# State passes of two mixers with their products grouped by rows, and a new order of steps for the second block

## What is computed

```python
def hgrn2_chunked(q, log_f, v):
    def step(state, inp):
        ...
        o = attn @ vt + jnp.einsum('bhtd,bhde->bhte', qt * jnp.exp(cum), state)
        ...
        state = jnp.exp(last[:, :, 0, :, None]) * state + jnp.einsum('bhsd,bhse->bhde', kt * jnp.exp(last - cum), vt)
        return state, o

def gated_delta_chunked(q, k, v, beta, g):
    def step(state, inp):
        u, w, qd, kd, qkc, gl = inp
        v_new = u - w @ state
        o = qd @ state + qkc @ v_new
        state = gl[..., None, None] * state + jnp.swapaxes(kd, -1, -2) @ v_new
        return state, o
```

## Time and profile before

| | |
|---|---|
| time, median of 3 runs | 4048.95 us (4043.9 to 4053.02) |
| the profiled execution | 4049.31 us, span of its instructions 4047.5 us |
| busy in that execution | PE 3833.2 us (95%), DVE 2624.0 (65%), ACT 1559.1 (39%), POOL 181.7 (4%) |
| mean granted PE clock | 0.968 of full speed |
| chain that ended last | PE 81%, DVE 11%, ACT 3%, DMA 2% |

### The profile page before, as it was taken

One profiled execution on the slowest core, in us unless ns is written; L12 is line 12 of the kernel. 1 busy time (PEld: TensorE's weight loads), 2 busy tenths in 40 slices (PEclk: granted clock), 3 DMA queues, 4 the chain that ended last, 5 costly groups with the idle time before them and its releaser, 6 DMA issues.

```text
span 4047.5 us, 49585 instructions
## 1 busy us (share of the span) xinstructions
PE 3833.2 (95%) x19548; PEld 3145.3 (78%) x19548; DVE 2624.0 (65%) x4164; ACT 1559.1 (39%) x2627; POOL 181.7 (4%) x335
## 2 busy tenths in 40 slices
PE   6889999998999999999989999999999989999998
PEld 5769878877788788887876788778888766887776
DVE  6887465655785522447778753776568788447865
ACT  3453232244532422334433343554334433335542
POOL 0000000000000000000111000000001110000010
PEclk9999899999998999999999999999899999999999
DMA  7502255532211332334444222134244442331233
GB/s 242 165 22 84 73 178 197 193 116 72 63 48 58 112 94 84 108 109 126 145 150 150 75 85 88 66 112 138 88 135 136 148 151 86 94 94 47 84 132 113
DMA packets 227128, 451.60 MB, mean 112 GB/s; under 512 B 18560, under 2 KB 63648, under 8 KB 225104
## 3 DMA queue, kind: packets, MB, share of 16 engines
q1 hardware_dynamic: 197584, 335.12, 25.6%
q0 software_dynamic: 29312, 113.32, 8.8%
HBM read 412.45 MB, written 35.93 MB: 111 GB/s over the span
## 4 chain that ended last, share of the span: by engine, by line
PE 81%; DVE 11%; ACT 3%; DMA 2%; issue 2%; SPq 0%; POOL 0%; DVEq 0%; ACTq 0%; POOLq 0%
PE ps L608 62%; PE ps L151 13%; PE ps L162 4%; DVE arena L173 3%; DVE arena L188 2%; ACT arena L247 2%; DVE spl L173 2%; DMA arena<-cumd 1%; DVE X L173 1%; DMA arena<-kvd 1%; PE ps L859 1%; DVE sm L194 1%; DVE arena L224 1%; PE ps L157 1%; ACT sph L247 0%
## 5 line engine op out<-in xcount | busy, mean ns | idle before, releaser
L173 DVE TENSOR_TENSOR spl<-ring,sph 128x1024 fp32r<-128x1024 f32 (+2 forms) x556 | 650.6, 1178 | 695.8 <-ACT sph L247 695.2
L247 ACT ACTIVATE sph<-ring 128x1024 fp32r<-128x1024 f32 (+2 forms) x556 | 558.5, 1018 | 692.4 <-PE ps L608 661.1
L608 PE MATMUL ps<-sph,HTh 128*128 128x512 f32 (+3 forms) x1680 | 666.0, 396 | 11.6 <-DVE HTl L173 5.0
L608 PE MATMUL ps<-spl,HTh 128*128 128x512 f32 (+3 forms) x1680 | 623.6, 371 | 0.0
L608 PE MATMUL ps<-sph,HTl 128*128 128x512 f32 (+3 forms) x1680 | 623.5, 371 | 0.0
L247 ACT ACTIVATE arena<-ps 128x512 f32<-128x512 f32 (+2 forms) x570 | 314.1, 564 | 763.4 <-PE ps L608 411.3
L608 PE MATMUL ps<-HTh,sph 128*128 128x512 f32 x1360 | 540.5, 397 | 11.3 <-ACT X L247 10.5
L608 PE MATMUL ps<-HTl,sph 128*128 128x512 f32 x1360 | 532.3, 391 | 0.0
L608 PE MATMUL ps<-HTh,spl 128*128 128x512 f32 x1360 | 532.3, 391 | 0.0
L151 PE MATMUL ps<-arena 128*128 128x128 f32 (+6 forms) x2264 | 369.6, 344 | 56.4 <-DVE arena L173 30.5
L608 PE MATMUL ps<-sph 128*128 128x512 f32 x992 | 400.5, 404 | 4.8 <-DVE spl L173 4.8
(11 more groups left out here) (218 smaller groups left out, 4898.8 us busy)
## 6 DMA issues: line engine op xcount, KB each, us to landing
ring<-in_w_in SPq DMA_DIRECT2D x264, 512.0 KB, 3.7
arena<-in_ada_w SPq DMA_DIRECT2D x88, 512.0 KB, 5.0
arena<-cumd POOLq DMA_DIRECT2D x128, 256.0 KB, 3.9
ring<-in_w_down SPq DMA_DIRECT2D x44, 512.0 KB, 3.7
ring<-in_w_gate SPq DMA_DIRECT2D x40, 512.0 KB, 3.7
ring<-in_w_up SPq DMA_DIRECT2D x40, 512.0 KB, 4.3
ring<-in_w_mem SPq DMA_DIRECT2D x32, 512.0 KB, 3.4
ring<-in_w_out SPq DMA_DIRECT2D x32, 512.0 KB, 3.6
```

The lines of the kernel that those rows point to most:

```text
L173: self.e.tensor_tensor(o, a, b, op).then_inc(*self.done.up())
L247: self.e.activation(o, a, f, **kw).then_inc(*self.done.up())
L608: ins = pe.e.matmul(o, l, r, start=k0 == 0 and i == 0 and not b.pairs, stop=k0 + b.ks == b.kt and i == 3 * b.ks - 1 and (c0 > 0 or not b.p ...
```

## The change

The functions `hgrn_pe` and `inv_pe` are changed, and the two strings of the second block. In both functions the products over 64 rows are taken together: the bank of the outputs is cleared by the product with one row of zeros, then come the two state products of the rows 0 to 63, then the four products over 128 rows, then the two of the rows 64 to 127, with a wait on the first two in place of `pe.own()`. In `inv_pe` the state part of the outputs moves ahead of the step of the weave, around `values_pe`, so that the bank og is taken earlier; after the step only the four state products and the four of G5 with VN are left. All sums have the same terms. The scores of "mix" stay as they are. The two strings of the second block have the same number of every letter but in another order.

```diff
     ("proj", 0):
-        "35McMdMd3Md8Md3M2d2Md2Mc4McMdc2Mcdc7M5c2M2dMcMsMcd2Mc5MscMdM2dMcdMdMc3Md6M2cMsdc2MdsMc4Mc2dcd2Mc2M2c"
...
+        "22Ms8Msd4M2d2McMcMcMd2Mc2Md5M2c5Md3Mc2dc3Md5Mc2dMc2dM2dcMc2Mcd2Mc3Md14M2c3Mc2McMdcMdsMdsd3c2MdMcdM2s"
...
     ("proj", 1):
-        "17Ms3MrMr2M2r7Msd6Md7MdMc6Mc3MdcMcMc2McMdcd2McMd5Md2MdM2cd3M2cd6Md3MdMcd2M2dcMcdMd2c5Md2McMc3Mc2d2sM"
...
+        "5M2r12Mr3Ms6Mr5Md4Mc7Mc3Mdc6MdMc2MdMcM2c2MdMc2Mc3Md3MdMd2Mdc2Md2c2M2dMd3Mc3M2c5Md3M2d2csc2MdMc3Mc3Md"
...
@@ hgrn_pe
+                    pe.e.matmul(b[:, 0:256], NFr[0][0:1, :], zero.to_broadcast([1, 256]), start=True, stop=False)
                     pe.wait_ge(at["st", l, c], at["lev_acc", l])
-                    for h in HO:
-                        pr, ti = (h % 2) * 64, h // 2
-                        hs = slice(64 * h, 64 * h + 64)
-                        if h == 1:
-                            pe.own()
-                        at["ob", l, c] = pe.mm(b[:, hs], [
-                            (ACC[:, c, h * 128:(h + 1) * 128], BV3[:, c, hs]),
-                            (BQ3[pr:pr + 64, ti, c * 128:(c + 1) * 128], STs[c % 2][pr:pr + 64, ti, :])])
+                    for half in range(2):
+                        if half:
+                            for h in range(4):
+                                hs = slice(64 * h, 64 * h + 64)
+                                pe.add(b[:, hs], ACC[:, c, h * 128:(h + 1) * 128], BV3[:, c, hs])
+                            pe.wait_ge(at["ob", l, c])
+                        for ti in range(2):
+                            pr, hs = 64 * half, slice(64 * (2 * ti + half), 64 * (2 * ti + half) + 64)
+                            at["ob", l, c] = pe.add(b[:, hs], BQ3[pr:pr + 64, ti, c * 128:(c + 1) * 128], STs[c % 2][pr:pr + 64, ti, :],
+                                                    stop=half + ti == 2)
@@ inv_pe
-                    if m < 3:
-                        values_pe(pe, l, m + 1)
+                    b2 = take(pe, ("og", l, m), pool("og"))
+                    pe.e.matmul(b2[:, 0:256], NFr[0][0:1, :], zero.to_broadcast([1, 256]), start=True, stop=False)
+                    for half in range(2):
+                        if half and m < 3:
+                            values_pe(pe, l, m + 1)
+                        pe.wait_ge(at["og", l, m] if half else None)
+                        for ti in range(2):
+                            pr, hs = 64 * half, slice(64 * (2 * ti + half), 64 * (2 * ti + half) + 64)
+                            at["og", l, m] = pe.add(b2[:, hs], QT_[pr:pr + 64, m, ti, :], SG[pr:pr + 64, ti, :])
                 yield (0.5, 0)
                 if m < 4:
-                    b2, b3 = [take(pe, (n, l, m), pool(n)) for n in ("og", "sg")]
+                    b3 = take(pe, ("sg", l, m), pool("sg"))
                     pe.wait_ge(at["vn", l, m])
...
-                    for h in HO:
-                        pr, ti = (h % 2) * 64, h // 2
+                    for h in range(4):
                         hs = slice(64 * h, 64 * h + 64)
-                        if h == 1:
-                            pe.own()
-                        at["og", l, m] = pe.mm(b2[:, hs], [
-                            (G5[:, m, h * 128:h * 128 + 128], VN[:, hs]),
-                            (QT_[pr:pr + 64, m, ti, :], SG[pr:pr + 64, ti, :])])
+                        at["og", l, m] = pe.add(b2[:, hs], G5[:, m, h * 128:h * 128 + 128], VN[:, hs], stop=h == 3)
```

More of the change, by code:

```diff
@@ new lines @@
+        "5Md5McsMdc2Md6McdcMd4Mc2MdMc2dMc2Md2Mcs2MsdMscdsMdMd4Ms2McMdMdMs3MdMc2McMd2s2Mc3McdMs2Md6Mcs3McMcdsc"
+        "dc2ds3Mc2Md3McMsdsc2Mc3Mdc4Ms4cMdMcMcscdMd2Md3M3dsMsdcMc2MsdM2c2Mc2Mc2dMdcs2M2sMsMs3MsMs4M2s2M2s3MsM"
+        "sMp3MsM2pMsM2psp3Ms3Mp2spsMp4Mps2MpMpM3ps2p2M2spMpMspMsMspMs2Ms2Mp2Mp2Msp2Mpsp2s5M3p2sMp3Mp2sMpMspMp"
+        "M2s2p2MsMspMpMsM2p2s2pMpM2p5Mpg3p2M4pM2p2MpMpM2pMpMpM2p2M3p2MgMpgM3p2MpM2p3MpM4pM3p4Mg19Mg4Mg4MgMg5M"
+        "g4MtMt2MtMt4Mg2MtM3tMt2Mt2M2t3Mt2Mt2M2t3Mt5Mt5MtMt2Mt2Mt2Mt3MtMt5Mt4Mt2Mt3Mt30M3t6Mt7Mf2M2f2MfMf5MfM"
@@ new lines @@
+        "2f2MfMf3Mf2Mf2MfMf3MfMfMfMfMf5MfMfMnfMf2M2f5Mn2Mf4MfMf3MnMf4Mf4MnMn2f2Mf2M2fM3fnxMnxyxMxyMxn2yxny2n"
+        "7M2yx4M2z2Mz2Mz4Mz29Mm12Mm2Mmsm3Mm28M",
+    ("proj", 1):
+        "5M2r12Mr3Ms6Mr5Md4Mc7Mc3Mdc6MdMc2MdMcM2c2MdMc2Mc3Md3MdMd2Mdc2Md2c2M2dMd3Mc3M2c5Md3M2d2csc2MdMc3Mc3Md"
+        "MdsMcMcdMdMsc3Ms3McdMd4MdMsd3MdMd2c3Mc2Mc3McdMcsd2cds2dcs5MdscMc3McsMcMd3Mscs6MdMs5Ms3d3Ms2d3Msd2sdc"
+        "McdMc4Msd3McMdMsd8MdMcMscMcMcMc2Mds3McMcMc2dcdMcMdMdsMc2dMdcMcd2MsdMcMsMcMdM3csMc2dsMs2M2s8MsMsMsMs"
+        "3M2s5M2s2p3MspMpsMpM2psMpMs2p2M2sMp2M2s2p6Msps2MpMpspMs2MpMsMpMrp3Mps2M2p2M2sp2MpMspMsM2p2Mp2s2M2p4M"
+        "sps3MpM2s2pMp2MpspsMpMs2ps8M4s2p2M2pM5pg3p2Mp3M2pg2pMpM3p5M2pMpM2pgpM3p2M2pgM5p2M3p14Mg7Mg5Mg9MgMt3M"
+        "t2MtMt4Mt2M3t4Mt4MtMt7M3tMtMt9Mgt3MtMt3M3t2Mt11MtMt2MtMt7MsM3t7Mt8Mg2Mt11Mt7M3f3Mf4Mf2MfMf2MfMfMf2Mf"
+        "MfMf2MfMfMf2MfMf2Mf2MfMf3Mnf4Mf5Mn2Mf4Mf3Mn2Mf3Mf2MfMf2MfMfn3MfnM2f3Mf3M3f2nx2MyMxnyx2ynx2n4Myx2My"
+        "10MxMyMx2M3zM2z26M2m17M2m4Mm25M",
```

10 lines of the change are left out of this document (removed).

## The result

| | before | after |
|---|---|---|
| time, median | 4047.99 us (4 runs) | 3999.15 us (3988.8 to 3999.68, 4 runs) |
| ratio | | 0.9873, 95% interval 0.9853 to 0.9892 |
| span of the profiled execution | 4047.5 us | 3997.2 us |
| mean granted clock in it | 0.968 | 0.974 |

What follows compares the result with a forecast made beforehand. PE was taken to bound the kernel, busy 95% of the span. Grouped products -8.5, scan order -12.9 and crowded pass steps +6.8 sum to -14.6 us: from 4049.3 to 4034.7, said as 4035 us, likely 4024 to 4045.

Steps and rivals of the forecast that it cites:

- (a): State passes: bank og is taken earlier, needing ACT's copy of the chunk before; 0.9 us to spare, costed at nothing.
- (b): State passes: PE needs DVE's next state; covered by 0.2 us only where no projection lies between; costed at nothing.
- (c): Grouped products: the wait on the first two is met, since five other products lie between (1.21 or 0.91 us).
- Part 1: Grouped products in hgrn and delta rule: about 0.5 us less in each of 16 chunks, -8.5 us with clock.
- the count: Second block's scan: 5.4 us row period minus PE's work, summed over short units from 8 on; 28.9 before, 16.0 after.
- Time saved on the other engines is worth nothing by itself: Whole kernel: an edit is worth only what it takes from PE's own stream or PE's waits.
- the relief of the scan: Second block's scan: the new orders cut the summed shortage from 28.9 to 16.0 us, worth -12.9 us.
- 28.9 against 43.5: Second block's scan: shortage counted before the change against PE time measured as empty in two windows, in us.
- the crowding: Second block's pass: steps beyond the second at a position go from 16 to 31, 0.45 us each, +6.8 us.
- part 1's tenth: Grouped products: a tenth added to 8.0 us because some chunks run at half clock, giving -8.5 us.
- Rival (A): Scan relieved in full: 19.4 us of waits, 6.5 of clock, 8.5 from grouped products; 4015 us, chance 0.2.
- the part on waits: Passage on waits that the grouped products add or move: three listed, costed at nothing, up to 3.6 us without cover.

## Why the prediction was wrong, point by point

**Right.** PE bounds the kernel, hgrn's chunk takes 2.89 us, the last block of the delta rule 1.3, and there are 16 instructions more. Layer 1 is the one that gained. The waits (a), (b) and (c) appear nowhere. The Trainium skill's rule (TensorEngine Tiling (Array Packing), Key Properties) that a change of the tiling mode drains the engine fits the chunk: 0.53 us less with four changes fewer.

**Right by luck.** Part 1: -8.5 were forecast, and -6.5 ± 2.4 measured at equal clock. But its halves, priced at some 4 us each, are not alike: hgrn's gives -7.7 ± 2.4, the delta rule's 1.2 ± 3.2 the wrong way. Layer 0: the count said -1.0, measured are 1.1 ± 3.3 for its string. Place by place it was otherwise, by the profiles of layer 1's string alone and of both strings, which differ in layer 0's string only: from position 100 to 285 the new one takes 11.6 us less, from 285 to 330 3.5 more, and from 453 on 9.1 more. So the stretch with the scan gained over ten times what was counted, and the tail, which the prediction had cost at nothing, lost most of it. (A slip without weight: the steps r move by up to 16 positions, not 15.)

**Wrong, other engines.** "Time saved on the other engines is worth nothing by itself" doesn't hold in the scan: 22 us less of work on DVE gave 11.2. PE's waits there are waits for DVE, and a shorter queue on DVE shortens them though none of them names the operation that went.

**Wrong, the relief of the scan.** The step "28.9 against 43.5 ... it catches the place, if not all of it" is where it failed. I left the 12.9 us as counted. In layer 1, 27.5 us were empty between 180 and 285 and 17.6 were counted, and the new order took 23.8 of the 27.5 away. 5.4 of them went in the window 180 to 214, mostly the convolution's end, where the count had no shortage at all; what else it missed lies in the scan, where the run with less work on DVE points to DVE's own queue. -29.7 at equal clock stand against -11.9 counted for that layer.

**Wrong, the crowding.** +6.8 us was charged and next to nothing of it came: the window with eight steps at one place has 0.1 us empty in layer 1, the one of layer 0 0.9. With 33 more steps beyond the second the price came out as 0.34 each (0.45 charged), so the term was of the right kind, but it doesn't start with the first step.

**Left out, the clock.** The forecast held no term for it outside of part 1's tenth. After runs at 0.9745 for 0.9690, 15 us, of which some 5 can be chance. One piece can be told: in layer 1's windows 13.6 us at 1.2 GHz are gone. A second is likely, in the first block: up to the first product of the second block the profiles hold 147 us at 1.2 GHz on average with the old functions (126 to 164, 11 profiles) and 132 with hgrn grouped (120 to 143, 7 profiles). The ranges overlap, so it rests on means, and the clock of whole executions doesn't settle it: beside the executions of before that belong to them, both mixers grouped lie 0.0039 higher and hgrn alone 0.0014. Rival (A) had a term for the clock, at 6.5 us for the scan, and full relief; it was the nearest with 4015 us, and it too was short, as it had neither the head of layer 1 nor a change of the clock in the first block.

**The new wait** of the transposes, 3.2 us, was missed in the part on waits: I had listed who needs the results of the block that got shorter, and not who was covered by its length. The delta rule's part was to give about 4 us, and with 3.2 of waits against them it shows nothing; but taking two of the three waits away gave nothing that could be measured either, so that this is the whole reason is not shown.

**Open.** Which hand-over makes the letters s and p need each other, place by place; and whether the grouped products raise the clock of the first block, and by which way.

## What to carry to other kernels

When a static count of waits covers two thirds of the empty time that the profile shows, look for the other third before pricing an edit; scaling the count to the whole would have given 19.4 us here and still been short. Where all engines share one order, the worth of a part of it can't be read from the part: here gains of stretches added in one layer and not in the other, and gains of single streams gave 6 us where both at once gave 17.6. So compare whole orders by their measured times, and give the clock of each execution beside its time. When an experiment lengthens one transfer, look at what the others did too. When a block on the critical engine is made shorter, ask what its length was hiding.

## What the runs showed of the hardware

Two transfers of 64 bytes from DRAM to DRAM in POOL's queue, repeated ahead of each unit's second row, made the 256 KB transfers of that queue land 3.2 us later (7.3 for 4.1 us) and the 512 KB transfers of SyncE's queue 3.1 us later (7.7 for 4.6) in the same stretch. The kernel took 113 us more in all. A load a quarter as large landed only 0.8 us sooner (3.6 for 4.4 us in the same kernel). An exponential over 128x128 took 0.39 us with a bias for each row and 0.30 with none. A clear by one row over 256 columns takes 0.30 us between products over other rows, at either side.
